# Score products of the second block's gated recurrence in fewer, narrower levels, and its gated linear recurrence with the decay gates ahead of the input gates

## The reference, cut to what matters

```python
S_t = diag(f_t) @ S_{t-1} + k_t v_t^T
o_t = S_t^T q_t
```

```python
r  = sigmoid(uc @ wa + ba)          # decay gate
ig = sigmoid(uc @ wx + bx)          # input gate
a  = exp(-8 * r * softplus(-lam))
h_t = a_t * h_{t-1} + sqrt(1 - a_t**2) * (ig_t * uc_t)
out = (h * gelu(y)) @ w_out
```

## Time and profile before

| what | value |
|---|---|
| median of 3 runs | 1138.95 us |
| the profiled execution's own time | 1138.59 us |
| its span (first to last instruction) | 1137.4 us |
| TensorE busy | 1122.9 us, 99% |
| DVE busy | 660.1 us, 58% |
| ACT busy | 574.5 us, 51% |
| POOL busy | 297.1 us, 26% |
| mean granted TensorE clock | 0.998 of full |
| HGRN2's score levels, from the first product to the last | 544.8 to 646.3 us |
| RG-LRU's gates to the start of its output product | 883.3 to 920.9 us |

### The profile page before, as it was taken

One profiled execution on the slowest core, in us unless ns is written; L12 is line 12 of the kernel. 1 busy time (PEld: TensorE's weight loads), 2 busy tenths in 40 slices (PEclk: granted clock), 3 DMA queues, 4 the chain that ended last, 5 costly groups with the idle time before them and its releaser, 6 DMA issues.

```text
span 1137.4 us, 19300 instructions
## 1 busy us (share of the span) xinstructions
PE 1122.9 (99%) x8117; PEld 1044.9 (92%) x8117; DVE 660.1 (58%) x1039; ACT 574.5 (51%) x878; POOL 297.1 (26%) x193
## 2 busy tenths in 40 slices
PE   8999999999999999999999999999999999999997
PEld 7899989999989999889998889999889979999986
DVE  6755765677675454338897665343238797434324
ACT  6646555555454644436732445444335855544432
POOL 3022100000005444422421114444510003444440
PEclk9999999999999999999999999999999999999999
DMA  8679474554647666655543358665556255765550
GB/s 273 205 250 326 141 241 138 175 153 134 209 151 211 180 188 201 203 185 153 186 165 112 111 164 268 210 189 189 191 180 188 91 182 152 218 189 187 187 183 37
DMA packets 155152, 207.48 MB, mean 182 GB/s; under 512 B 9471, under 2 KB 128409, under 8 KB 155066
## 3 DMA queue, kind: packets, MB, share of 16 engines
q1 hardware_dynamic: 151274, 193.11, 54.2%
q0 software_dynamic: 3792, 13.15, 3.5%
HBM read 205.01 MB, written 4.24 MB: 184 GB/s over the span
## 4 chain that ended last, share of the span: by engine, by line
PE 89%; DVE 7%; ACT 3%; issue 1%; DMA 0%; POOL 0%; SPq 0%; DVEq 0%; ACTq 0%
PE bank L492 18%; PE bank L495 18%; PE bank L500 18%; PE bank L520 9%; PE bank L516 9%; PE bank L512 9%; PE bank L861 3%; DVE wlo L1359 2%; PE bank L787 1%; PE bank L797 1%; ACT whi L958 1%; DVE area L1507 1%; PE bank L562 1%; PE bank L809 1%; DVE uc L1507 0%
## 5 line engine op out<-in xcount | busy, mean ns | idle before, releaser
L1359 DVE TENSOR_TENSOR wlo<-raw,whi 128x1024 fp32r<-128x1024 f32 x275 | 336.2, 1250 | 232.4 <-ACT whi L958 231.6
L958 ACT ACTIVATE whi<-raw 128x1024 fp32r<-128x1024 f32 x362 | 360.5, 1044 | 113.8 <-PE bank L520 107.1
L1947 POOL TENSOR_TENSOR wlo<-raw,whi 128x1024 fp32r<-128x1024 f32 x87 | 223.2, 2565 | 253.8 <-ACT whi L958 253.8
L492 PE MATMUL bank<-hh,whi 128*128 128x256 f32 x1784 | 285.1, 281 | 0.0
L495 PE MATMUL bank<-hh,wlo 128*128 128x256 f32 x1784 | 281.7, 279 | 0.0
L500 PE MATMUL bank<-hl,whi 128*128 128x256 f32 x1784 | 281.5, 279 | 0.0
L492 PEld LDWEIGHTS bank<-hh,whi 128*128 128x128 f32 x1784 | 241.4, 188 | 3.3 <-issue 2.7
L495 PEld LDWEIGHTS bank<-hh,wlo 128*128 128x128 f32 x1784 | 240.8, 188 | 0.0
L500 PEld LDWEIGHTS bank<-hl,whi 128*128 128x128 f32 x1784 | 240.6, 188 | 0.0
L1954 POOL TENSOR_TENSOR st<-st,half 128x1 f32<-128x1 f32 x18 | 10.8, 609 | 334.0 <-DVE st L1376 301.8
L512 PE MATMUL bank<-whi,gh 128*128 128x512 f32 x264 | 81.4, 390 | 0.0
(11 more groups left out here) (313 smaller groups left out, 1225.7 us busy)
## 6 DMA issues: line engine op xcount, KB each, us to landing
raw<-in_ffn_w_in SPq DMA_DIRECT2D x88, 512.0 KB, 3.8
raw<-in_w_in SPq DMA_DIRECT2D x72, 512.0 KB, 4.8
raw<-in_ffn_w_out SPq DMA_DIRECT2D x44, 512.0 KB, 3.3
raw<-in_hgrn_w_in SPq DMA_DIRECT2D x32, 512.0 KB, 4.2
raw<-in_w_ffn_gate SPq DMA_DIRECT2D x22, 512.0 KB, 4.7
raw<-in_w_ffn_up SPq DMA_DIRECT2D x22, 512.0 KB, 4.3
raw<-in_w_ffn_down SPq DMA_DIRECT2D x22, 512.0 KB, 3.3
raw<-in_w_branch SPq DMA_DIRECT2D x16, 512.0 KB, 4.4
```

The lines of the kernel that those rows point to most:

```text
L492: T.matmul(out, wh[:, i, c], xh[:, k, :], start=first and (i, k) == pairs[0], stop=False)
L958: A.activation(half_of(whi, j, h), half_of(raw, j, h), ACT.Copy).then_inc(s_hi[j % NS][h], 1)
L1359: V.tensor_tensor(half_of(wlo, j, h), half_of(raw, j, h), half_of(whi, j, h).bitcast(f32), ALU.subtract).then_inc(s_lo[j % NS][h], 1)
L1947: G.tensor_tensor(half_of(wlo, j, 1), half_of(raw, j, 1), half_of(whi, j, 1).bitcast(f32), ALU.subtract).then_inc(s_lo[j % NS][1], 1)
```

## The change

The levels of HGRN2 go from nine to eight per pair. The new level 0 holds both the diagonal and the pairs of neighbours (m = 1): ACT writes silu(q) into a spare part of `hn` (`pair_q`: 192 columns per head and tile), DVE writes behind it the 64 odd tokens of q times their rate, and after that all of q times its rates into `qT` (`with_rates`). TensorE multiplies k by all 192 columns, one bank per head, so the first level takes two bank turns. DVE copies it out in four instructions: per head 128 columns x 2 for the diagonal, then, after a wait for its own instruction, 64 columns x 2 for the neighbours. Levels 1 to 6 have m = 2 to 64, and multiply k only by those 64 of the 128 columns of q that the level keeps (`second_halves`); their copy is 128x256. Level 7 is the cross tile level. No level is left for the slot "rest", which goes. `lev` shrinks to 128x576.

In RG-LRU the order of the gates is (1,0), (1,1), (1,2), (0,0), (1,3), (0,1), (0,2), (0,3), as (i, n). DVE multiplies the decay gates by the channel's rate in two instructions of 128x1024 (`rate`), so that Tanh and Exp are two instructions of 128x1024 each in place of eight of 128x256. The first two scans go ahead of the splits of `use(("ly", 1))`.

The placement and the two helpers:

```diff
+        GATES = [(1, 0), (1, 1), (1, 2), (0, 0), (1, 3), (0, 1), (0, 2), (0, 3)]
...
+        def pair_q(j):
+            return hn_flat[:, 768 * (j % 2):768 * (j % 2) + 768].rearrange("p (i n) -> p i n", n=192)
...
+        def second_halves(z, m):
...
+            return z.rearrange("p (n w) -> p n w", w=2 * m)[:, :, m:2 * m]
...
-                if at_level[j] < 9:
+                if at_level[j] < 8:
```

TensorE:

```diff
+            def first_level(j):
+                tq.wait_ge(s_k, j + 1)
+                tq.wait_ge(s_pq, j + 1)
+                for h in range(2):
+                    b = turn(("lev", j, 0, h), 4 + side[0] % 4)
+                    side[0] += 1
+                    tq.wait_ge(*free(("lev", j, 0, h)))
+                    for t in range(2):
+                        tok = T.matmul(banks[b][:, 192 * t:192 * t + 192], kT[:, 2 * j + h, 128 * t:128 * t + 128], pair_q(j)[:, 2 * h + t, :],
+                                       start=True, stop=True)
+                    tok.then_inc(s_full[b], 1)
...
+                        c, at_ = slice(128 * t, 128 * t + 128), 64 * (2 * h + t)
+                        tok = T.matmul(banks[b][:, at_:at_ + 64], k[:, c], second_halves(q[:, c], 2 ** i), start=True, stop=True)
...
             turn_outputs((0, 1))
-            levels("rest")
             outputs(1)
...
-            lru_gates(0)
-            lru_gates(1)
+            for i, n in GATES:
+                lru_gate(i, n)
```

ACT:

```diff
             def q_of(j):
-                qj = qT[:, 2 * j:2 * j + 2, :]
                 aq.wait_ge(*evac("col", "hq", j))
-                A.activation(qj, qj, ACT.Silu).then_inc(s_q0, 1)
+                if j >= 2:
+                    aq.wait_ge(*full("lev", j - 2, 0, 1))
+                A.activation(pair_q(j)[:, :, 0:128], qT[:, 2 * j:2 * j + 2, :].rearrange("p k (t n) -> p (k t) n", n=128),
+                             ACT.Silu).then_inc(s_q0, 1)
...
             def tangents(h):
-                for c in range(4 * h, 4 * h + 4):
-                    aq.wait_ge(*evac("lg", 1, c // 2))
-                    A.activation(th[:, c, :], rg[:, c, :], ACT.Tanh, scale=vec[:, 120 + c:121 + c])
+                sl = slice(4 * h, 4 * h + 4)
+                aq.wait_ge(s_rate, h + 1)
+                A.activation(th[:, sl, :], rg[:, sl, :], ACT.Tanh)
...
             def decays(h):
-                for c in range(4 * h, 4 * h + 4):
-                    A.activation(aT[:, c, :], rg[:, c, :], ACT.Exp, scale=vec[:, 96 + c:97 + c]).then_inc(s_aa, 1)
+                sl = slice(4 * h, 4 * h + 4)
+                A.activation(aT[:, sl, :], rg[:, sl, :], ACT.Exp, scale=-1.0).then_inc(s_aa, 1)
...
-            lru_gates(0)
+            for i, n in GATES[:4]:
+                lru_gate(i, n)
             use(("ly", 0))
             tangents(0)
-            lru_gates(1)
+            for i, n in GATES[4:6]:
+                lru_gate(i, n)
             tangents(1)
+            for i, n in GATES[6:]:
+                lru_gate(i, n)
             decays(0)
             decays(1)
```

DVE:

```diff
+            def with_rates(j):
...
+                qj, fj = (z[:, 2 * j:2 * j + 2, :].rearrange("p k (t n) -> p (k t) n", n=128) for z in (qT, fT))
+                pq = pair_q(j)
+                vq.wait_ge(s_q0, j + 1)
+                vq.wait_ge(s_f, j + 1)
+                V.tensor_tensor(pq[:, :, 128:192].rearrange("p i (n o) -> p i n o", o=1), pq[:, :, 0:128].rearrange("p i (n o) -> p i n o", o=2)[:, :, :, 1:2],
+                                fj.rearrange("p i (n o) -> p i n o", o=2)[:, :, :, 1:2], ALU.mult).then_inc(s_pq, 1)
+                rates_set[j] = own.mark(V.tensor_tensor(qj, pq[:, :, 0:128], fj, ALU.mult))
...
+                if i == 0:
+                    for h in range(2):
+                        b, out = bank_of("lev", j, 0, h), Ss[:, 4 * j + 2 * h:4 * j + 2 * h + 2, :]
+                        tile = b[:, 0:384].rearrange("p (t n) -> p t n", n=192)
+                        vq.wait_ge(*own.mark(V.copy_predicated(out, lev[:, 0:128].rearrange("p (o n) -> p o n", o=1).broadcast_to([128, 2, 128]),
+                                                               tile[:, :, 0:128])))
+                        V.copy_predicated(out.rearrange("p t (n w) -> p t n w", w=2)[:, :, :, 1], lev[:, 128:192].rearrange("p (o n) -> p o n", o=1).broadcast_to([128, 2, 64]),
+                                          tile[:, :, 128:192]).then_inc(evacuated("lev", j, 0, h), 1)
+                    return
+                vq.wait_ge(*(evac("lev", j, i - 1) if i > 1 else evac("lev", j, 0, 1)))
+                mask = lev[:, 128 + 64 * i:192 + 64 * i].rearrange("p (o n w) -> p o n w", o=1, w=m).broadcast_to([128, 4, 64 // m, m])
+                V.copy_predicated(Ss[:, 4 * j:4 * j + 4, :].rearrange("p i (n w) -> p i n w", w=2 * m)[:, :, :, m:2 * m], mask,
+                                  bank_of("lev", j, i)[:, 0:256].rearrange("p (i n w) -> p i n w", i=4, w=m)).then_inc(evacuated("lev", j, i), 1)
...
             for j in range(1, 4):
+                with_rates(j - 1)
                 use(("hf", j))
...
+                        if (name, g2, part) == ("hv", 0, 0):
+                            with_rates(3)
                         use((name, g2, part))
...
+            def rate(h):
...
+                sl = slice(4 * h, 4 * h + 4)
+                for n in (2 * h, 2 * h + 1):
+                    vq.wait_ge(*evac("lg", 1, n))
+                V.tensor_tensor(rg[:, sl, :], rg[:, sl, :], vec[:, 120 + 4 * h:124 + 4 * h].rearrange("p (c o) -> p c o", o=1).broadcast_to([128, 4, 256]),
+                                ALU.mult).then_inc(s_rate, 1)
...
+            rate(0)
             use(("lu", 3))
+            rate(1)
             gated_input(0)
...
-            use(("ly", 1))
             scan(0)
             scan(1)
+            use(("ly", 1))
```

More of the change, by code:

```diff
@@ L40, in shape_constants @@
     t = np.arange(128)[None, :]
-    masks = [((s // (2 * m) == t // (2 * m)) & (s % (2 * m) < m) & (t % (2 * m) >= m)) for m in LEVELS]
-    masks.append(s == t)
-    lev = np.stack(masks, axis=1).astype(np.int32)
+    lev = [s == t]
+    for m in LEVELS:
+        mask = (s // (2 * m) == t // (2 * m)) & (s % (2 * m) < m)
+        lev.append(mask[:, t[0] % (2 * m) >= m])
+    lev = np.concatenate(lev, axis=1).astype(np.int32)
     return oh, hsel, np.ascontiguousarray(lev)
@@ L144, in build @@
         og = sbuf(hg, "og", [128, 2, 1024])
-        lev = sbuf(hg, "lev", [128, 8, 128], i32)
+        lev = sbuf(hg, "lev", [128, 576], i32)
         nw = sbuf(hg, "nw", [128, 128])
@@ L459, in build @@
                     advance((name, g2, part), range(4))
[L460 to L464, removed]
+                    assert (name, g2, part) != ("hv", 1, 0) or min(at_level[0:2]) == 8
+        assert min(at_level) == 8
+        lev_q = {ji: i + 1 for i, ji in enumerate(ji for ji in sorted(level_no, key=level_no.get) if ji[1] < 7)}
         def evacuated(*key):
@@ L841, in tensor_program @@
             feed_forward(0, 2, 3)
+            def first_level(j):
[9 more added lines that the diff above has]
+                    tok.then_inc(s_full[b], 1)
             def level(j, i):
+                if i == 0:
+                    first_level(j)
+                    return
                 b = turn(("lev", j, i), 4 + side[0] % 4)
                 side[0] += 1
[L847 to L852, removed]
-                tq.wait_ge(*free(("lev", j, i)))
[L854 to L861, removed]
+                tq.wait_ge(s_q, lev_q[j, i - 1])
+                tq.wait_ge(*free(("lev", j, i)))
+                for h in range(2):
+                    k, q = kT[:, 2 * j + h, :], qT[:, 2 * j + h, :]
+                    if i == 7:
+                        tok = T.matmul(banks[b][:, 128 * h:128 * h + 128], k[:, 0:128], q[:, 128:256], start=True, stop=True)
+                        continue
+                    for t in range(2):
+                        c, at_ = slice(128 * t, 128 * t + 128), 64 * (2 * h + t)
+                        tok = T.matmul(banks[b][:, at_:at_ + 64], k[:, c], second_halves(q[:, c], 2 ** i), start=True, stop=True)
                 tok.then_inc(s_full[b], 1)
@@ L916, in tensor_program, with lru_gate @@
             feed_forward(1, 5, 6)
-            def lru_gates(h):
+            def lru_gate(i, n):
+                h = n // 2
                 tq.wait_ge(s_gw, 128)
[L921 to L930, removed]
+                b = turn(("lg", i, n), next_bank())
+                tq.wait_ge(s_conv, 8 + 2 * n + 2)
+                tq.wait_ge(*free(("lg", i, n)))
+                for dd in range(2):
+                    c, out = slice(256 * i + 128 * dd, 256 * i + 128 * dd + 128), banks[b][:, 256 * dd:256 * dd + 256]
+                    for k in (2 * n, 2 * n + 1):
+                        tok = T.matmul(out, gw[:, h, k - 4 * h, c], uc[:, k, :], start=k == 2 * n, stop=k == 2 * n + 1)
+                tok.then_inc(s_full[b], 1)
             project_pair([("lu", 0), ("lu", 1)], 6)
```

(26 more changed lines are left out.)

23 lines of the change are left out of this document (11 added, 12 removed).

## The result

The changed kernel takes 1141.28 us (median of 15 runs, 1139.41 to 1142.94) where before takes 1138.7 (median of 15); the ratio is 1.002, with a 95% interval of 1.0012 to 1.0027. It is slower, by 2.6 us, about 0.2%. The profiled execution took 1141.99 us, 3.4 more than the profiled one of before.

What follows compares the result with a forecast made beforehand. TensorE's own work was taken as the bound, busy 1122.9 of 1137.4 us. Levels -2.0, new wait +1.7, end of HGRN2 0 and recurrence -0.6 summed to -0.9: 1138.0 us on the 1138.95 median, range 1135.7 to 1140.8.

Steps and rivals of the forecast that it cites:

- The price of a product: TensorE score products: a floor of 0.1115 us per record, also for 64 columns, and 0.160 us for 192 columns.
- The forecast of -2.0 on TensorE's own work: HGRN2 score levels: minus 2.0 us on TensorE, all because a pair has one level fewer.
- The place of the new wait: Slot hv00: five bank turns in a rotation of four, so (3, 0)'s second head waits for DVE to free (0, 5)'s bank.
- Its length: TensorE's wait in slot hv00: plus 1.7 us, bounded by 0 from below and 4.9 from above.
- DVE's lateness: DVE before slot hv00: reaches the slot's scores 2.74 us later, at 587.8 instead of 585.08.
- The copy's row: DVE's narrower score copies: 0.63 us for 512 columns, taken as 0.36 for 256 and 0.23 for 128.
- Rival (b): DVE much later at slot hv00: a wait of 4.9 us, sum +2.3, 1141.3 us; chance 0.06.
- The end of HGRN2: Last unit and outputs: 0.35 us of waits go, a 0.3 us wait for ACT's evacuation comes; zero in sum.
- The recurrence: RG-LRU: the factor starts 0.6 us earlier, shortening TensorE's waits at its end; minus 0.6 us.
- (a): DVE on time at slot hv00: wait under 0.4 us, sum -2.6, 1136.3 us; chance 0.25.
- (c): Score products reading q with gaps are slow, 0.213 us a record: +16 us, 1154 us; chance 0.03.
- (d): No floor under a record, narrow score products cost by column, 0.053 us: 11 us less, 1127 us; chance 0.03.

Runs made afterwards that it cites:

- best: Changed kernel without pair 0's level in slot hv00, pair 3's rates ahead of the x steps, ACT's last cross-level copy behind its evacuations: 1136.13 us against before's 1138.95.
- x_behind: Changed kernel with DVE's four steps on x moved behind slot hv00's levels, all five bank turns kept: 1137.0 us, ratio 0.9984 to before.
- levels_only: Kernel before with only the HGRN2 part of the change, the recurrence left as before: 1141.88 us, ratio 1.0024 to before.
- wait_before: Kernel before with one TensorE wait added ahead of pair 3's level 0 in slot hv00, products and copies unchanged: 1142.76 us against 1138.95.
- full_width: Changed kernel without pair 0's level in slot hv00, and levels 1 to 6 multiplying all 128 columns of q: 1137.07 us, ratio 0.9985 to before.

## Why the prediction was wrong, point by point

**The price of a product** was right. 0.160 for 192 columns: the three first levels ahead of hv00 took 1.22 us more, 1.16 were forecast. 0.1115 for 64: 0.110 measured. The forecast of -2.0 on TensorE's own work holds: +1.22 + 0.39 - 3.50 = -1.9, with the waits at the end in it, and -2.3 in best, where they are gone.

**The place of the new wait** was right: the second head of (3, 0), on the bank of (0, 5), freed by DVE. **Its length** was mis-sized, 1.7 forecast against 2.58. The step that was off is DVE's lateness, forecast as 2.74 and measured as 4.03 (its first multiply in the slot starts at 589.11 against 585.08). 0.2 of it is the later start of the whole stage. The first levels took 2.2 each, not 2.10. The larger part is in the later levels, taken as 1.02 each. Two of them, in the timeline of DVE:

```profile
565.11 0.42 DVE L1825 TENSOR_TENSOR qT<-qT,tot 128x256 f32<-128x256 f32 x1
565.44 0.42 DVE L1826 TENSOR_TENSOR kT<-kT,tot 128x256 f32<-128x256 f32 x1
565.78 0.74 DVE L1840 COPY_PREDICATED Ss<-lev,bank 128x256 f32<-128x256 int32 x1
566.30 0.47 DVE L1807 TENSOR_TENSOR hn<-hn,fT 128x256 f32<-128x256 f32 x1
...
572.97 0.42 DVE L1826 TENSOR_TENSOR kT<-kT,tot 128x256 f32<-128x256 f32 x1
573.31 0.44 DVE L1840 COPY_PREDICATED Ss<-lev,bank 128x256 f32<-128x256 int32 x1
573.64 0.50 DVE L1825 TENSOR_TENSOR qT<-qT,tot 128x256 f32<-128x256 f32 x1
```

The copy of the level with m = 2 lasts 0.74 us, as long as the 512-column copy of before; with m = 4 and more, 0.44. From one start to the next it is 0.52 in place of 0.33. That happens to each of the four pairs, three of them ahead of hv00: 3 x 0.2 = 0.6 us. The rest came in one level that ran beside POOL's products (0.3 us longer). The copy's row had been scaled by its columns alone.

**What follows the wait** was missed altogether, and it is the step that put the result outside the range. The sum charged a wait at its own length and put the clock's price at nothing. With the wait of 2.6 us alone the time would have been about 1139.6, by x_behind's 1137.0, inside the range of 1135.7 to 1140.8. The clock's fall added about 1.7 us to the median (1141.28 against 1139.6) and 2.7 to the profiled execution. The trace of before has no wait of TensorE over 1 us behind its first 8 us, with the clock at 1.00 through the levels, so it showed no price for one; but a sum that puts a stall of 1.7 us, bounded by 4.9, into an engine that never stands still would have had to carry that price as an unknown term with an upper bound. Rival (b) came out near the measured time, 1141.3 us, by luck: it needed a wait of 4.9 us, and there was one of 2.6.

**The end of HGRN2**: a wait of 0.3 for ACT's evacuation was forecast, 0.27 measured. **The recurrence**: -0.6 forecast, -0.4 measured. It was late by the start of `rate(1)`, which DVE began 0.1 to 0.2 later than worked out; the pause behind it was right. Rivals (a), (c) and (d) are refuted by the traces, (a) as the state of things, though x_behind comes near the time that it gives: 1137.0 against the 1136.3 worked out.

With measured terms the sum is -1.9 + 2.6 + 2.9 - 0.4 = +3.2, against +3.3 in the span; the 2.9 are the clock's 2.7 and the 0.2 by which the wait is longer than its idle time.

## What to carry to other kernels

A wait put on an engine that never waits is to be charged at its own length, and the clock's price is to stand beside it as a term that may come: here a wait of 1.3 us cost about 1.3, one of 2.6 cost 4.3 in the medians and 5.5 in the profiled execution. Where between the two the fall sets in, no run shows. Before work is split into more bank turns, count the turns of each slot against the rotation, and ask who frees the bank within that slot. Where the pitch no longer falls with the columns, as here between 128 and 64, fewer products help and narrower ones don't.

## What the runs showed of the hardware that was not expected

The clock falls with one wait of 2.6 us in a stream that had kept TensorE busy for hundreds of us. When it falls differs, 1.4 to 1.5 us after TensorE's last result in levels_only and the changed kernel, and in wait_before 3.0 us after it, with TensorE back at work. Its stay at half differs too: 6.8 us in the first two traces, 3.4 us in wait_before's. By their times, some executions of either length of wait seem to go the other way. A masked copy on DVE (COPY_PREDICATED, 128x256 from PSUM) takes 0.74 us when it writes in runs of two float32, and 0.44 in runs of four and more; the 128x128 copies that write every second column last 0.44 too (0.25 from one start to the next). That the short runs are the cause was read from the four levels with m = 2 against the 20 others, and not tried by itself. How the bank is read doesn't show: packed in the changed kernel 0.74, in runs of two in full_width 0.75. The multiplies in the same levels, with the same runs, are not slower (0.42).
